# First norm's weights read in 16-byte pieces onto the feature partitions, first up weights with four neighbouring rows a partition, one row load and two filler matmuls changed at the start

## What is computed

```python
def rms_norm(x, g):
    xf = x.astype(jnp.float32)
    y = xf * lax.rsqrt(jnp.mean(xf * xf, axis=-1, keepdims=True) + NORM_EPS)
    return (y * g.astype(jnp.float32)).astype(x.dtype)

def swiglu_ffn(h, w_up, w_down):
    gate, up = jnp.split(h @ w_up, 2, axis=-1)
    return (jax.nn.silu(gate) * up) @ w_down
...
    for l in range(DEPTH):
        x = x + 0.5 * swiglu_ffn(rms_norm(x, norm_ffn1[l]), ffn1_up[l], ffn1_down[l])
        h = rms_norm(x, norm_mix[l])
        proj = h @ w_in[l]
...
    return rms_norm(x, final_norm)
```

## Time and profile before

| | us |
|---|---|
| median of three runs | 1087.44 (1087.03 to 1087.96) |
| the profiled execution's own time | 1087.18 |
| its span, first to last instruction | 1085.5 |
| PE busy in that span | 1077.3 |
| from the span's start to the first product on real data (line 1795) | 5.79 |
| from the span's start to chunk 1's first product | 20.12 |

### The profile page before, as it was taken

One profiled execution on the slowest core, in us unless ns is written; L12 is line 12 of the kernel. 1 busy time (PEld: TensorE's weight loads), 2 busy tenths in 40 slices (PEclk: granted clock), 3 DMA queues, 4 the chain that ended last, 5 costly groups with the idle time before them and its releaser, 6 DMA issues.

```text
span 1085.5 us, 15382 instructions
## 1 busy us (share of the span) xinstructions
PE 1077.3 (99%) x5276; PEld 902.9 (83%) x5276; DVE 891.1 (82%) x1174; ACT 652.2 (60%) x832; POOL 79.3 (7%) x102
## 2 busy tenths in 40 slices
PE   9999999999999999999999999999999999999997
PEld 6888888988988888888888888888899888888886
DVE  6989988766987698988889988986679877988895
ACT  6656654656954565665565755746469446565664
POOL 0034410100300000000000000001012000000000
PEclk9999999999999999999999999999999999999999
DMA  9576584754455555655646567648444554646651
GB/s 291 179 234 222 169 312 162 253 164 126 161 186 170 169 193 193 207 179 194 222 143 216 179 205 264 235 122 280 143 141 158 194 180 150 224 166 197 223 167 68
DMA packets 140091, 207.38 MB, mean 191 GB/s; under 512 B 5208, under 2 KB 103584, under 8 KB 139536
## 3 DMA queue, kind: packets, MB, share of 16 engines
q1 hardware_dynamic: 137600, 197.15, 55.0%
q0 software_dynamic: 2144, 9.12, 2.5%
q10 hardware_dynamic: 304, 0.53, 0.1%
HBM read 205.60 MB, written 1.05 MB: 190 GB/s over the span
## 4 chain that ended last, share of the span: by engine, by line
PE 93%; ACT 3%; DVE 1%; issue 1%; DMA 1%; SPq 1%; POOL 0%; POOLq 0%
PE psum L1704 30%; PE psum L1706 30%; PE psum L1705 30%; PE psum L1803 2%; PE psum L1722 1%; ACT xs L878 1%; DMA raw<-ffn_up_dram 1%; ACT w_hi L690 1%; SPq L488 0%; DVE w_lo L1079 0%; PE psum L2011 0%; ACT scores L890 0%; ACT pair L873 0%; ACT L978 0%; ACT xT L873 0%
## 5 line engine op out<-in xcount | busy, mean ns | idle before, releaser
L1079 DVE TENSOR_TENSOR w_lo<-raw,w_hi 128x1024 fp32r<-128x1024 f32 (+4 forms) x281 | 412.9, 1494 | 77.0 <-ACT w_hi L690 76.1
L1704 PE MATMUL psum<-w_hi,xT 128*128 128x512 f32 (+2 forms) x984 | 383.1, 389 | 0.2 <-DVE w_lo L1079 0.2
L1706 PE MATMUL psum<-w_hi,xT 128*128 128x512 f32 (+2 forms) x984 | 379.3, 385 | 0.0
L1705 PE MATMUL psum<-w_lo,xT 128*128 128x512 f32 (+2 forms) x984 | 379.0, 385 | 0.0
L690 ACT ACTIVATE w_hi<-raw 128x2048 fp32r<-128x2048 f32 (+5 forms) x167 | 284.5, 1709 | 72.4 <-PE psum L1706 66.7
L1704 PEld LDWEIGHTS psum<-w_hi,xT 128*128 128x128 f32 x984 | 184.7, 188 | 40.5 <-DVE w_lo L1079 2.0
L1706 PEld LDWEIGHTS psum<-w_hi,xT 128*128 128x128 f32 x984 | 184.7, 188 | 37.1
L1705 PEld LDWEIGHTS psum<-w_lo,xT 128*128 128x128 f32 x984 | 184.9, 188 | 34.4 <-issue 0.2
L807 ACT ACTIVATE oT<-xs 128x1024 fp32r<-128x1024 f32 x72 | 76.5, 1062 | 70.0 <-DVE xs L1079 70.0
L775 ACT ACTIVATE scores<-psum,stat 128x256 f32<-128x256 f32 x88 | 41.2, 473 | 110.9 <-PE psum L1706 110.0
L1079 DVE TENSOR_TENSOR oT<-xs,oT 128x1024 fp32r<-128x1024 f32 x72 | 88.0, 1229 | 0.0
(11 more groups left out here) (235 smaller groups left out, 1406.8 us busy)
## 6 DMA issues: line engine op xcount, KB each, us to landing
raw<-ffn_up_dram SPq DMA_DIRECT2D x170, 512.0 KB, 4.9
raw<-ffn_down_dram SPq DMA_DIRECT2D x44, 1024.0 KB, 4.8
raw<-w_in_dram SPq DMA_DIRECT2D x20, 1024.0 KB, 5.3
raw<-w_attn_proj_dram SPq DMA_DIRECT2D x8, 1024.0 KB, 5.0
raw<-w_out_dram SPq DMA_DIRECT2D x8, 1024.0 KB, 5.1
raw<-w_uq_dram SPq DMA_DIRECT2D x8, 576.0 KB, 4.0
gates<-b_gate_dram POOLq DMA_DIRECT2D x4, 1024.0 KB, 7.5
raw<-w_ukv_dram SPq DMA_DIRECT2D x8, 512.0 KB, 3.9
```

The source lines that it names most:

```text
L1079: return dve.tensor_tensor(dst, a, b, ALU.subtract)
L1704: nc.tensor.matmul(dst, a_hi, b_hi, start=first, stop=False)
L1705: nc.tensor.matmul(dst, a_hi, b_lo, start=False, stop=False)
L1706: return nc.tensor.matmul(dst, a_lo, b_hi, start=False, stop=last)
```

## The change

- The 1024 weights of the first norm are loaded straight to `gain_T`, four neighbouring weights to a partition: 256 pieces of 16 bytes, on ACT's DMA queue. The row load, PE's transpose of it, ACT's copy and their three semaphores are gone. DVE waits for the DMA itself.
- Feature 512h + 4p + k now lies on partition p, in block k. So every up-weight load of layer 0's first block takes rows 4p to 4p + 3 of a half for partition p (before: rows p, 128 + p, 256 + p, 384 + p), and the first tiles of x are transposed by columns that lie four elements (16 bytes) apart.
- The load of x tile (0,1) stands behind piece 2 instead of piece 1.
- `KEEP` is 1 instead of 3.

```diff
-WARM, KEEP = 4, 3
+WARM, KEEP = 4, 1
...
-        first_gain = gain[0:KD, 0:P]
...
             def load_up(L, f, q, r, j, a, room=None):
 
-                src = ups[f][L, a * 4 * P:(a + 1) * 4 * P, :].rearrange("(k p) (u n) -> p k u n", p=P, u=2)
+                rows = "(p k) (u n) -> p k u n" if (L, f) == (0, 0) else "(k p) (u n) -> p k u n"
+                src = ups[f][L, a * 4 * P:(a + 1) * 4 * P, :].rearrange(rows, p=P, u=2)
...
             def load_first(a):
 
-                src = ups[0][0, a * 4 * P:(a + 1) * 4 * P, :].rearrange("(k p) (u n) -> p k u n", p=P, u=2)
+                src = ups[0][0, a * 4 * P:(a + 1) * 4 * P, :].rearrange("(p k) (u n) -> p k u n", p=P, u=2)
                 dst = raw[:, a, :].rearrange("p (k u n) -> p k u n", k=4, u=2)
                 for k in range(4):
                     sp.dma_start(dst[:, k], src[:, k, :, 0:CH]).then_inc(first_landed[a][k], 16)
-                    if (a, k) == (0, 1):
+                    if (a, k) == (0, 2):
                         sp.dma_start(x[:, 1, half(0)], x_in[0, blk(1), half(0)]).then_inc(x_landed[0][1], 16)
...
                 act.sem_inc(w_hi_done.sem, 1)
-                act.wait_ge(gain_turned, 1)
-                act.activation(gain_T, psum[:, 1, 0:KD], ACT.Copy).then_inc(gain_kept, 1)
                 first_squares(0, 0)
...
-            act.dma_start(first_gain, gains[0:1, :].rearrange("o (k n) -> (o k) n", k=KD)).then_inc(gain_row_landed, 16)
+            with nc.allow_non_contiguous_dma(reason="1024 weights"):
+                act.dma_start(gain_T.rearrange("p (h k) -> p h k", h=2),
+                              gains[0:1, :].rearrange("o (h p k) -> (o p) h k", h=2, p=P)).then_inc(gain_T_landed, 16)
...
-                dve.wait_ge(gain_kept, 1)
+                dve.wait_ge(gain_T_landed, 16)
...
             def turn_first(h, t):
                 pe.wait_ge(x_landed[h][t], 16)
-                if (h, t) == (0, 0):
-                    tiles(psum[:, ALONE_BANK, :], x[:, 0, 0:P], 1).then_inc(first_turned, 1)
-                    tiles(psum[:, NORM_T_BANK[0][0], P:], x[:, 0, P:4 * P], 3, norm_tr)
-                else:
-                    tiles(psum[:, NORM_T_BANK[h][t], :], x[:, t, half(h)], 4, norm_tr)
+                columns = x[:, t, half(h)].rearrange("p (n k) -> p k n", k=4)
+                for k in range(4):
+                    alone = (h, t, k) == (0, 0, 0)
+                    bank = ALONE_BANK if alone else NORM_T_BANK[h][t]
+                    last = nc.tensor.transpose(psum[:, bank, k * P:(k + 1) * P], columns[:, k, :], ident[:, :])
+                    if alone:
+                        last.then_inc(first_turned, 1)
+                last.then_inc(norm_tr.sem, 1)
...
             turn_first(0, 0)
-            pe.wait_ge(gain_row_landed, 16)
-            nc.tensor.transpose(psum[:, 1, 0:KD], first_gain, ident[0:KD, 0:KD]).then_inc(gain_turned, 1)
             keep_clock(5, KEEP)
```

More of the change, by code:

```diff
@@ L240, in trunk @@
         x_landed = [[sem(f"x_landed{h}{t}") for t in range(TB)] for h in range(2)]
-        ones_set, ident_set, gain_row_landed = sem("ones_set"), sem("ident_set"), sem("gain_row_landed")
-        warm_set, gain_turned, gain_kept = sem("warm_set"), sem("gain_turned"), sem("gain_kept")
+        ones_set, ident_set, gain_T_landed = sem("ones_set"), sem("ident_set"), sem("gain_T_landed")
+        warm_set = sem("warm_set")
         first_sq, first_part = sem("first_sq"), sem("first_part")
```

## The result

The changed kernel takes 1089.0 us (median of 22 runs, 1087.69 to 1090.72), the kernel before beside it 1087.49 (22 runs, 1086.9 to 1088.76). The ratio is 1.0014, with a 95% interval of 1.0008 to 1.0019: slower, but by less than 0.2%. The time lies in the range given; the likeliest case, 1087.7, is missed by 1.3 us, and its mechanism did not happen.

The account below looks back on a forecast made before the run. Transfers bound the start, with PE 0.39 us behind, and PE bounds the rest. The small packets' +0.29 on 1087.18 gave 1087.5 against the profiled execution, 1087.7 for a median; range 1087.0 to 1089.2 with the stepped transposes.

Parts of the forecast that it names:

- Transfers bound the start, PE 0.39 behind: Start of chunk 1: PE waits until 20.12 us for the load's chain, and would itself have been free at 19.73.
- The row order of the up weights costs nothing: Loads of up weights, first eight and in the loop: packets stay equal, so picking every fourth row costs nothing.
- The rival on slow loads: First eight loads: every-fourth-row reads are slow, chunk 1's load lands about 2 us later, 1089.5 and more; chance 0.04.
- The gain's road: Norm's weights at the start: without transpose and copy, PE's first product comes at 5.3 to 5.8 us, which buys nothing.
- The exchange of piece 2 and x tile (0,1): Second block: the tile lands at 7.8 us, PE's transposes start 0.34 later behind a new wait, hidden under chunk 1's load.
- The small packets: The 256 gain pieces at 18 ns each delay chunk 1's load by 0.29 us (0 to 0.75).
- Two fillers fewer: PE from 4.83 to 5.79 us: taking them away costs no time in itself, but they may have held up the clock.
- the clock rises late: Rival at PE's start: low clock over one block gives 1088.2 (chance 0.04), over two blocks 1090.3 (chance 0.04).
- filler and first products 0.43 apart: Sign in the timeline after, for 512 columns on PE, that would show the clock is late.
- The stepped transposes: PE's transposes of x from columns 16 bytes apart: taken as no cost, because the same number of columns is read.
- the rival that had been given 0.20: Stepped transposes of x on PE are slow, 0.43 to 0.68 more a tile, time 1088.6 to 1089.3; chance 0.20.
- The loop's loads: Up-weight loads in the loop: new row order costs nothing, issued 10.6 us before ACT reads them; no new PE waits.

Follow-up runs that it names:

- e6_loads_alone: Kernel before with only the up weights of layer 0's first block loaded as four neighbouring rows a partition; 1088.82 us beside 1087.36, ratio 1.0011.
- e3_pieces_alone: Kernel before with the norm's weights loaded in 16-byte pieces, PE's transpose and ACT's copy of them removed; 1086.88 us beside 1087.19, ratio 0.9997.
- e5_hold: Changed kernel with SP's first weight load held until DVE has set the fillers' operand; 1088.2 us beside 1087.36 for the kernel before, ratio 1.0008.
- e8_warm7: Changed kernel with 7 fillers ahead of x tile (0,0) instead of 4; 1087.33 us beside 1087.36 for the kernel before, ratio 1.0002.
- e2_order_alone: Kernel before with only x tile (0,1) loaded behind piece 2 instead of piece 1; 1087.45 us beside 1087.19, ratio 1.0001.
- e1_keep_alone: Kernel before with only KEEP at 1 instead of 3; 1087.18 us beside 1087.19, ratio 1.0004.
- e4_layout_alone: Kernel before with up weights as four neighbouring rows a partition and x transposed by columns four elements apart; 1089.03 us beside 1087.19, ratio 1.0016.
- e11_uneven: Kernel before with the first eight weight loads taking their second half from column 2688 instead of 2816; 1089.01 us beside 1087.2, ratio 1.0018.

## Why the prediction was right and wrong, step by step

**Transfers bound the start, PE 0.39 behind: right of before, wrong of after.** The chain after has no load in it. The distance of 0.39 was read correctly (the books above close with it), but with so little between them both roads had to be watched, and the sum put the whole risk on the load's.

**The row order of the up weights costs nothing: this is the step that failed.** The sum put it at nothing "by the equal packets". That looked at what the weights' packets cost themselves. The cost was on a transfer beside them, on another queue: x tile (0,0), which the prediction took as through at 3.5, landed at 5.02. e6_loads_alone carries +1.46 of +1.5. The rival on slow loads had the right part but the wrong place: full queues until 15 us still moved 348 GB/s, nearly the 359 of the earlier trace rows; what lost was the stretch from 2 to 4 us. What PE waits for there is the tile alone, with nothing ahead of its transposes at about 3.6 but fillers.

**The gain's road: right that it buys nothing, wrong in the reason for its time.** DVE's first product was forecast at or before 5.3 and came at 5.74. With a punctual tile and old loads it was 5.12 (e3_pieces_alone), with the weights held back 4.28 (e5_hold). So with the old loads the removed steps save nothing: the pieces land as late as the copy had ended.

**The exchange of piece 2 and x tile (0,1): landing about right, the wait never seen.** The tile was forecast to land at 7.8. It is issued at 2.38 in the changed kernel and lands 5.3 later, at about 7.7; PE comes to it only at 9.89, since the clock is low. In e8_warm7, with the clock up, it lands at about 7.6, and the transposes start at 8.01 without a wait, right behind PE's own products. With the old loads (e2_order_alone) it lands later, at about 8.1. So neither the changed kernel nor e8_warm7 shows the wait of 0.34 that the sum put on PE's road. The exchange alone (e2_order_alone) moved no median by an amount that can be told.

**The small packets: over-sized.** The traffic of 4.5 to 5 us in the changed kernel, where ACT's queue carries hardly anything else:

```profile
q10 hardware_dynamic: 79, 0.00, 9.8%
```

0.098 x 16 x 500 / 79 = 9.9 ns each, not 18; 256 of them are 0.16 us of all engines, not 0.29. ACT took chunk 1's load 0.2 later in e8_warm7 (16.02) and 0.3 earlier in e3_pieces_alone than before (15.83), so even 0.16 can't be told from how executions differ. The Trainium skill ("DMA: Bandwidth & Descriptors", Specifications) says that transfers below 512 bytes don't reach line rate, because of a read-modify-write. The trace agrees on the rate: 16 bytes in 9.9 ns are about a fourteenth of what 1 KB in 47 ns moves. But the prediction took from it a price near the upper 47 ns a packet, and that is not borne out; whether a read-modify-write takes place, no run shows.

**Two fillers fewer: right,** as far as the medians tell, that it costs nothing (e1_keep_alone), and right that what they might hold up is the clock. The rival "the clock rises late", given 0.08 in two sizes (1088.2 and 1090.3), is what happened, and 1089.0 lies between them. It was held unlikely because PE had no gap as long as 1 us; with the late tile it had one of 1.44, and e2_order_alone's profile shows that a gap of 0.22 doesn't exclude a rise near 10 us. The size of the term is right (1.68 + 0.16 against the 1.72 worked out for one block); what set it off is the tile and not the fillers: with KEEP at 1 and a punctual tile nothing was lost, with KEEP at 3 and a late one (e6_loads_alone) nearly all. The sign that the prediction gave for it, "filler and first products 0.43 apart", was misread for the products: their records stand 0.43 apart at the full clock and 0.85 at the low one.

**The stepped transposes: right.** 0.04 a tile, far under the 0.43 to 0.68 of the rival that had been given 0.20. The Trainium skill ("Advanced Engine Details and Errata", SBUF Cachelines) has a penalty for an access to another line each time; what these transposes show of it is 0.47 against 0.43 for four.

**The loop's loads: right.** PE's distance to the kernel before is 1.7 at 51 us and 1.8 at 1072 us.

**The bounds.** The range held by luck: it had been drawn out to the stepped transposes, for a cost that didn't come, and another of like size took its place. "Within 0.2%" was right, at 1.4 thousandths, with the same luck.

**Still open:** why loads of uneven pitch delay the tile; and what moves the rise of the clock between executions, with or without an idle stretch. Neither e8_warm7 nor e3_pieces_alone is faster than the kernel before by an amount that was measured, so there is no version to recommend over it. Whether more fillers would also give back the loss with the old gain load and order (e4_layout_alone, e6_loads_alone, e11_uneven) was not tried.

## What to carry to other kernels

A transfer whose bytes and packets stay the same can still cost time on another one in flight beside it, so look at what else is on its way when the source pattern of a load changes, and at who waits for that with no cover. Where PE waits for its first data, try filling the whole of the wait, with room for data that come late: here three more fillers gave back all of the 1.5 us. Where two roads end within 0.4 us of each other, work out both with each of their inputs late.

## What the runs showed of the hardware

- The queue's time for issuing a weight load of 256 pieces of 1 KB depends on where the pieces lie: the first two take 1.31 us with one even pitch (before), and 0.97 with rows at every fourth place (e6_loads_alone) or with one half shifted by 512 bytes (e11_uneven). With the shorter issue the engines moved less in 2 to 4 us (0.38 MB in the changed kernel, against 0.59), and x tile (0,0) landed up to 1.5 us later.
- Packets of 16 bytes took 9.9 ns of an engine each (changed kernel, 4.5 to 5 us), next to 47 ns for 1 KB (before).
- The moment of the clock's rise differs between executions of kernels that keep PE nearly equally busy: the first four product records took 1.88 in the profiled execution before, 2.63 in e3_pieces_alone, 3.38 in e2_order_alone, at medians within 0.6 us. The granted clock is printed as 1.00 in the low stretches too.
- The matmul behind PE's wait at 20.12 took 0.50 us instead of 0.39, and the next one started 0.34 behind it instead of 0.23. So a wait that goes gives back 0.11 on top of its length.
- Four transposes with columns 16 bytes apart took 0.47 us, with neighbouring columns 0.43.
